# Hybrid decoder trunk on one core: the remainder of a weight unit written by one GpSimd operation of 512 columns instead of two of 256

## The reference

```python
for l in range(DEPTH):                       # DEPTH = 2
    h = rmsnorm(x, norm_mix[l])
    x = x + hybrid_mixer(h, w_in[l], ...)    # mLSTM | GLA | S5 | HGRN2 branches, gates, w_branch, w_out
    h = rmsnorm(x, norm_xattn[l])
    x = x + cross_attention(h, rmsnorm(mem, norm_mem[l]), xattn_w_q[l], xattn_w_kv[l], xattn_w_o[l])
    h = rmsnorm(x, norm_mlp[l])
    x = x + sq_relu_mlp(h, mlp_w1[l], mlp_w2[l])
return rmsnorm(x, norm_final)
```

## Time and profile before

| what | value |
|---|---|
| median of 3 runs | 1982.82 us (1982.56 to 1984.0) |
| the profiled execution | 1982.35 us |
| its span, first to last instruction | 1980.6 us |
| TensorE busy | 1960.2 us (99%), 11851 matmuls |
| VectorE busy | 960.5 us (48%) |
| ScalarE busy | 910.9 us (46%) |
| GpSimd busy | 1077.2 us (54%), 1348 instructions |
| read from HBM | 184.51 MB, 95 GB/s over the span |
| granted TensorE clock, mean | 0.998 of full speed |

### The profile page before, as it was taken

The page is one execution under the profiler, slowest core; times in us unless marked ns, Lnnn a source line. Parts: engine busy times, 40 slices in busy tenths (PEclk is TensorE's granted clock), DMA queues, the critical chain, the costliest instruction groups (busy, mean ns, idle before and its releaser), DMA issues.

```text
span 1980.6 us, 30676 instructions
## 1 busy us (share of the span) xinstructions
PE 1960.2 (99%) x11851; PEld 1617.7 (82%) x11851; DVE 960.5 (48%) x1429; ACT 910.9 (46%) x1553; POOL 1077.2 (54%) x1348
## 2 busy tenths in 40 slices
PE   8999999999999999999999999999999999999998
PEld 6788788878888888888887887887898888888887
DVE  5887778846143321211258787786631532211212
ACT  6755555345445442423355546353553544333323
POOL 4564554846835454646465555368385445545451
PEclk9999999999999999999999999999999999999999
DMA  6422333323422333333333233233343233333331
GB/s 178 116 77 76 84 82 92 96 92 108 148 86 80 97 97 96 96 98 99 96 98 80 74 88 81 76 100 83 107 138 112 74 93 99 97 96 96 97 100 70
DMA packets 196654, 190.72 MB, mean 96 GB/s; under 512 B 23642, under 2 KB 190108, under 8 KB 196124
## 3 DMA queue, kind: packets, MB, share of 16 engines
q1 hardware_dynamic: 196508, 188.76, 32.5%
HBM read 184.51 MB, written 3.15 MB: 95 GB/s over the span
## 4 chain that ended last, share of the span: by engine, by line
PE 92%; DVE 4%; ACT 3%; issue 1%; DMA 0%; SPq 0%; DVEq 0%; ACTq 0%
PE gemm L636 84%; PE mix L636 7%; DVE work L1788 1%; DVE work L1797 1%; ACT w_hi L1305 1%; PE mix L1201 0%; DMA w_raw<-in_w_in_dram 0%; DVE gate_t L1797 0%; DVE h_lo L1797 0%; PE mix L1107 0%; DVE work L2179 0%; ACT work L1421 0%; ACT work L1420 0%; ACT work L1781 0%; PE mix L810 0%
## 5 line engine op out<-in xcount | busy, mean ns | idle before, releaser
L629 POOL TENSOR_TENSOR w_lo<-w_raw,w_hi 128x256 fp32r<-128x256 f32 x672 | 559.6, 833 | 875.2 <-ACT w_hi L1305 874.8
L636 PE MATMUL gemm<-work_split,w_hi 128*128 128x512 f32 (+1 forms) x2048 | 599.2, 376 | 0.0
L636 PE MATMUL gemm<-h_hi,w_hi 128*128 128x512 f32 x1440 | 569.6, 396 | 1.4 <-DVE h_lo L1797 1.4
L630 POOL TENSOR_TENSOR w_lo<-w_raw,w_hi 128x256 fp32r<-128x256 f32 x672 | 563.1, 838 | 0.0
L636 PE MATMUL gemm<-h_hi,w_lo 128*128 128x512 f32 x1440 | 560.9, 390 | 0.0
L636 PE MATMUL gemm<-h_lo,w_hi 128*128 128x512 f32 x1440 | 560.8, 389 | 0.0
L1305 ACT ACTIVATE w_hi<-w_raw 128x512 fp32r<-128x512 f32 x672 | 382.7, 623 | 236.1 <-DMA w_raw<-in_mlp_w_dram 186.2
L636 PEld LDWEIGHTS gemm<-work_split,w_hi 128*128 128x128 f32 x2048 | 375.6, 188 | 70.2 <-issue 0.3
L636 PE MATMUL gemm<-work_split,w_lo 128*128 128x512 f32 (+1 forms) x1024 | 384.9, 376 | 0.0
L636 PEld LDWEIGHTS gemm<-h_hi,w_hi 128*128 128x128 f32 x1440 | 270.2, 188 | 67.1 <-issue 7.0
L636 PEld LDWEIGHTS gemm<-h_hi,w_lo 128*128 128x128 f32 x1440 | 270.3, 188 | 56.9
(11 more groups left out here) (307 smaller groups left out, 1636.5 us busy)
## 6 DMA issues: line engine op xcount, KB each, us to landing
w_raw<-in_mlp_w_dram SPq DMA_DIRECT2D x256, 256.0 KB, 2.6
w_raw<-in_w_in_dram SPq DMA_DIRECT2D x208, 256.0 KB, 2.7
w_raw<-in_xattn_w_kv_dram SPq DMA_DIRECT2D x64, 256.0 KB, 2.9
w_raw<-in_w_branch_dram SPq DMA_DIRECT2D x32, 256.0 KB, 2.6
w_raw<-in_w_out_dram SPq DMA_DIRECT2D x32, 256.0 KB, 2.6
w_raw<-in_xattn_w_q_dram SPq DMA_DIRECT2D x32, 256.0 KB, 2.8
w_raw<-in_xattn_w_o_dram SPq DMA_DIRECT2D x32, 256.0 KB, 2.6
w_raw<-in_w_in_dram SPq DMA_DIRECT2D x32, 128.0 KB, 3.5
```

What stands on the lines that cost most here:

```text
L629: pool.tensor_tensor(lo[:, 0:half], raw[:, 0:half], hi[:, 0:half].bitcast(F32), ALU.subtract)
L630: pool.tensor_tensor(lo[:, half:], raw[:, half:], hi[:, half:].bitcast(F32), ALU.subtract).then_inc(split_ready, 1)
L636: return pe.matmul(o, w, a, start=start, stop=stop, skip_group_check=True)
```

## The change

For each unit, the two GpSimd operations on the left and the right 256 columns become one on all 512. The remainder is the same, the wait for `split_hi` stands before it as it did, and `split_ready` is signalled by it. Nothing else differs; GpSimd's 1344 tensor operations become 672, and the program of the other four engines is unchanged apart from line numbers, which fall by two behind this place.

```diff
             for u in range(ALL_UNITS):
                 raw, hi, lo = unit_at(u)
                 pool.wait_ge(split_hi, u + 1)
-                half = raw.shape[-1] // 2
-                pool.tensor_tensor(lo[:, 0:half], raw[:, 0:half], hi[:, 0:half].bitcast(F32), ALU.subtract)
-                pool.tensor_tensor(lo[:, half:], raw[:, half:], hi[:, half:].bitcast(F32), ALU.subtract).then_inc(split_ready, 1)
+                pool.tensor_tensor(lo, raw, hi.bitcast(F32), ALU.subtract).then_inc(split_ready, 1)
```

## The result

The changed kernel takes 1999.95 us in the median of 4 runs (1998.59 to 2001.07), the kernel before 1982.79 us (1982.56 to 1984.0). The ratio is 1.0085, with a 95% interval of 1.0073 to 1.0097: 17.2 us slower, where +0.7 us was forecast. The profiled execution has a span of 1998.8 us against 1980.6 us.

The account below looks back on a forecast made before the run. TensorE was taken to bound the kernel, busy 1960.2 of 1980.6 us, with GpSimd off the path. Terms of +0.3 (squares) and +0.4 us (sixth `h_lo`), others zero, made 1982.82 + 0.7 = 1983.5 us; range 1981.2 to 1986.3.

Parts of the forecast that it names:

- Place 1: Last addition of squares, 30.56 us: VectorE meets a longer GpSimd exclusion, TensorE gets the result 0.3 us later.
- ends of its sum: Margins for the sixth `h_lo` (0.4 us either way), mixer's scores (0.4) and mLSTM part (0.8): sum -0.9 to +2.3.
- the sum for a unit is the same, 0.84 us: VectorE's dense stretches: one 512-column exclusion of 0.84 us equals two of 0.42, fewer collisions but each twice as long.
- place 2: Sixth `h_lo`, 49.64 us: +0.4 us (0 to 0.8) before TensorE's wait, 0.4 us less behind it.
- place 3: Mixer's scores, 110.38 us, chain from VectorE to TensorE: 0, with 0.4 us to either side.
- place 4: mLSTM part, 258.07 us, both layers, TensorE waits for ScalarE, which waited for VectorE: 0, up to 0.4 us either way each.
- the clock one: Slower rival: longer TensorE standstill at 50.80 us brings another half-clock stretch (1.9 us); +4.2 us, 1987.0 us, chance 0.07.
- The Trainium skill's rule: Faster rival: GpSimd blocks VectorE for its whole instruction, 1.48 us a unit becoming 1.25; gain past 0.2%, chance 0.03.

Follow-up runs that it names:

- rest behind each unit: Against the kernel before: one 512-column operation per unit, then four small input-less GpSimd writes (first 100 units of each layer except 7 and 8); 1993.91 us, ratio 1.0061.
- rests behind 256 columns: Against the kernel before: two small input-less GpSimd writes after each 256-column operation (first 100 units of each layer except 7 and 8); 1987.07 us, ratio 1.0024.

## Why the prediction was wrong

**What held.** The new operation alone is 1.26 us (1.25), its mean 1424 ns (1350 to 1450), GpSimd's busy time 938.6 us (900 to 980). A unit that is ready earlier was worth nothing, TensorE never waited for `w_lo`, and the MLP kept its 178 matmuls. The place was right as well: VectorE's collisions on the path of the first 110 us, with VectorE's operations at about 1.6 us. Place 1 went the way it was described, at twice the size: the last addition of squares took 1.27 us, and TensorE's wait for it grew from 1.15 to 1.85 us, +0.7 instead of +0.3. The rows of the changed kernel (VectorE, then TensorE):

```profile
30.86 1.27 DVE L1786 TENSOR_TENSOR work<-work,gate_t 128x512 f32<-128x512 f32 x1 [0.47 <-ACT gate_t L1315]
```

```profile
32.27 1.02 PE L634 MATMUL mix<-consts_sb,work 128*128 128x1 f32 x8 [1.85 <-DVE work L1786]
```

Two smaller slips stand in the prediction: half of the ends of its sum is 0.8 us and not 0.9 (the range would end at 1986.2), and the full list of TensorE's waits before has ScalarE in it too, 2.6 us in four places, and not VectorE alone.

**The step that failed** is the sentence "Where VectorE has its next operation always at hand, the sum for a unit is the same, 0.84 us", with what hangs on it: the "0.4 us less behind it, once the backlog is gone" of place 2, the zero of place 3 and the zero of place 4.

1. *The size.* I added 0.42 + 0.42. The runs give the time that a VectorE operation waits behind 128, 256, 384 and 512 columns as 0.14, 0.42, 0.70 and 0.97 us: 0.28 us for each 128 columns, less 0.14 us once for each collision. Merging two collisions pays that credit once instead of twice. I had a row for 256 columns only and drew the line through zero. From the slope the second half is 0.55 us, and the rows left room for it: an operation starts 0.70 us after the one before and 0.10 us is what one column costs, so up to 0.60 us go with the columns, not 0.42.
2. *The number.* Held against the shortest record of the same operation over all eleven kernels, VectorE's operations lost 114 us in the kernel before and 168 us in the changed one. In sums of a unit that is 114 / 0.84 = 136 units and 168 / 0.97 = 174 units. The size accounts for 136 x 0.13 = 18 of the 54 us, the other 36 us are more units that meet VectorE at all. Counted one by one, 307 VectorE operations lost more than 0.1 us before and 212 in the changed kernel, where half of 307 would be 154. Why they meet more often is argued and not shown: in a dense stretch GpSimd gets through a whole unit for each VectorE operation, every 1.70 us (45.28, 46.98) instead of every 2.3, and what it thereby brings forward could have run while VectorE waits, or beside operations that it doesn't hold up. So it isn't "given back", because the later part was free. The rest behind each unit, which undoes this haste, brought the count down to 198 only, so this is at most a part of the reason.
3. *Where it counts.* I priced four places and took the rest as covered, as TensorE showed no wait there. The cover was thin: a wait of zero in the trace says nothing of how close it was. In the changed kernel TensorE waits for VectorE at 91.28 (1.96 us), at 225.99 (1.15 us, a row "issue"); the rows added up above count 21 places, their like before 9. The kernel lost about a third of the 54 us more on VectorE.

Of the rivals the clock one had the nearest mechanism: two more stretches at half clock, 3.3 us, not one of 1.9. It needed all signs at once in my account, and its 1987.0 us was still 13 us short of the measured time. The Trainium skill's rule, that the loser waits for the whole instruction (SBUF — State Buffer, "SBUF: two separate sides"), would have made the change a gain; the runs show waits of 0.14 us behind an operation of 0.46 and 0.97 us behind one of 1.26. What the trace agrees with is the Trainium skill's figure for a two-input operation of GpSimd, 2.6 cycles an element at 1.2 GHz (GPSIMD Engine Reference, "Elementwise — side-by-side cycle accounting"): 2.17 ns, and the slope here is 0.55 us for 256 columns, 2.15 ns.

**What stays open.** The share of turns and of size in the 17.2 us isn't separated: the rest behind each unit gave back 6 us, 496 + 16 columns 5.3 us, and in both the profiled execution also has fewer stretches at half clock than the changed kernel's. Whether the remaining 11 to 12 us are all due to the 0.13 us a unit wasn't shown by itself, and the slower kernel with rests behind 256 columns says that the place of a collision matters as well as their number. Each kernel has one trace, and whether a stretch at half clock follows a standstill can differ between kernels with the same program up to there, so a single stretch (1.6 to 1.9 us) is no firm part of a difference.

## What to carry to other kernels

When two engines exclude each other operation by operation, the length of an operation acts like a priority: in this kernel the engine off the path did best with short ones where the engine on the path is dense, and long ones cost nothing elsewhere. It holds until its own fixed cost for an operation makes it late, so cut finely by place and not everywhere. To price a change to such an engine, read the busy time of its neighbour, count how many of its operations are hit, and fit its waits at two lengths, since one row can't tell slope from offset; and take a wait of zero for unknown slack, not for cover.

## What the runs showed of the hardware

- A VectorE operation with two SBUF inputs (128x512 float32, 0.69 us alone) behind a two-input GpSimd operation of 128, 256, 384 and 512 columns took 0.84, 1.11, 1.40 and 1.66 us.
- Small ones are hit as hard: a VectorE operation of 128x1 (line 2006 of the changed kernel) took 1.13 us, 0.58 us in the kernel before, and 0.16 us in its shortest record. So were those with scalars: the two of 128x1024 by a scalar at 58 us took 2.49 us together, 1.93 us before.
- VectorE operations with `gemm` as one of two inputs weren't held up: of the 96 of `x_t<-x_t,gemm` in the kernel before, 54 ran while GpSimd wrote a remainder, and all took 0.69 us.
- GpSimd's small writes without an input (128x32) didn't hold VectorE up: beside four of them, 0.67 us, `gate_t` took its 0.75 us.
- A remainder operation of GpSimd has a fixed part: 16 columns took 349 ns in the mean, with waits, and 128 columns 0.46 us in the median; nine of them in a row took 3.82 us (at 678 us), so four make a unit of about 1.7 us where one makes 1.26.
- The stretch at half clock behind TensorE's first wait (at about 33 us) is not a fixed part of the kernel: it is in the trace of before, and missing in the kernel with 512 columns in attention and MLP only, whose program is the same up to there and whose wait was as long (1.16 us, 1.15 before). Its time was no better for that, 1982.41 us: TensorE then waited 0.8 us for `w_lo` at 38 us, as in every traced kernel without that stretch (0.8 us in four of them, 1.97 us with four of 128 columns) and in none with it.
